# Long convolutions of a fused block: last frequency columns in four column groups of TensorE, 9-row products in the middle of each tile, odd halves first, and the inverse's 64-row products in both row halves

## What is computed

```
def fft_long_conv(u, spec, skip):
    L = u.shape[1]
    uf = u.astype(jnp.float32)
    y = jnp.fft.irfft(jnp.fft.rfft(uf, n=2 * L, axis=1) * spec[None], n=2 * L, axis=1)[:, :L]
    return (y + uf * skip.astype(jnp.float32)).astype(u.dtype)
...
    for n in range(HYENA_ORDER):
        gate = u[..., (n + 1) * D_HYENA:(n + 2) * D_HYENA]
        z = gate * fft_long_conv(z, spectra[:, n], skip[n])
```

## Time and profile before

| | us |
|---|---|
| median of three runs | 3216.32 (3215.01 to 3219.29) |
| the profiled execution, device time | 3212.31 |
| its span, first to last instruction | 3210.6 |
| TensorE busy in the span | 2982.2 (93%) |
| VectorE / ScalarE / GpSimd busy | 1142.0 / 779.5 / 900.5 |
| mean granted TensorE clock | 0.973 of full speed |

### The profile page before, as it was taken

How to read it: one execution, slowest core, us unless ns; L and a number is a source line. 1 busy time by engine, 2 the same in 40 slices (tenths; PEclk the granted TensorE clock), 3 DMA queues, 4 the chain that set the end, 5 groups by cost and what they waited for, 6 DMA issues and landing times.

```text
span 3210.6 us, 39686 instructions
## 1 busy us (share of the span) xinstructions
PE 2982.2 (93%) x15996; PEld 1985.1 (62%) x15996; DVE 1142.0 (36%) x1865; ACT 779.5 (24%) x1104; POOL 900.5 (28%) x744
## 2 busy tenths in 40 slices
PE   6999999999999999999999999999888888888887
PEld 4777778878788667887779794455333333333333
DVE  4566585661620154224152675513111011111112
ACT  2435542232322233223143621111000000000001
POOL 2342534455354314444424230001111111111110
PEclk9999999999999999999999999999999999899999
DMA  7324354542222212223312121047999999999997
GB/s 260 92 80 134 130 183 170 196 135 76 86 92 93 78 40 79 92 92 111 86 53 87 42 85 56 1 170 274 407 413 423 411 407 416 403 413 402 409 404 291
DMA packets 256000, 631.61 MB, mean 197 GB/s; under 512 B 19217, under 2 KB 208690, under 8 KB 230525
## 3 DMA queue, kind: packets, MB, share of 16 engines
q1 hardware_dynamic: 245053, 619.23, 51.6%
q0 software_dynamic: 10240, 8.43, 0.8%
q10 hardware_dynamic: 576, 2.10, 0.2%
HBM read 633.88 MB, written 20.97 MB: 204 GB/s over the span
## 4 chain that ended last, share of the span: by engine, by line
PE 63%; DMA 19%; DVE 6%; issue 5%; PEld 3%; ACT 2%; POOL 2%; SPq 0%; PEldq 0%; DVEq 0%; POOLq 0%; ACTq 0%
DMA arena<-in_w_up 18%; PE ps L545 12%; PE ps L547 12%; PE ps L546 11%; PE ps L4277 9%; PE ps L3480 2%; POOL ring_parts L427 2%; PE ps L3710 1%; PE ps L4294 1%; PE ps L2520 1%; PE ps L2519 1%; PE ps L2518 1%; PEld ps L545 1%; PEld ps L547 1%; PE ps L2670 1%
## 5 line engine op out<-in xcount | busy, mean ns | idle before, releaser
L427 POOL TENSOR_TENSOR ring_parts<-ring,arena_parts 128x512 fp32r<-128x512 f32 x544 | 720.7, 1358 | 1006.6 <-ACT arena_parts L401 772.5
L545 PE MATMUL ps<-arena_parts,arena_parts 128*128 128x512 f32 (+1 forms) x2012 | 749.7, 373 | 8.3 <-DVE arena_parts L536 4.2
L547 PE MATMUL ps<-arena_parts,ring_parts 128*128 128x512 f32 (+1 forms) x2012 | 741.2, 368 | 0.0
L4277 PE MATMUL ps<-arena 128*64 128x512 f32 x1008 | 500.1, 654 | 140.3 <-DMA arena<-in_w_up 95.4
L546 PE MATMUL ps<-hT_parts,arena_parts 128*128 128x512 f32 (+1 forms) x1648 | 596.0, 362 | 0.0
L4278 PE MATMUL ps<-arena 128*64 128x512 f32 x1008 | 501.3, 655 | 0.0
L4277 PEld LDWEIGHTS ps<-arena 128*64 128x64 f32 x1008 | 146.1, 150 | 462.5 <-issue 460.7
L545 PEld LDWEIGHTS ps<-arena_parts,arena_parts 128*128 128x128 f32 x2012 | 378.5, 188 | 85.2 <-issue 7.5
L547 PEld LDWEIGHTS ps<-arena_parts,ring_parts 128*128 128x128 f32 x2012 | 378.9, 188 | 69.1
L401 ACT ACTIVATE arena_parts<-ring 128x2048 fp32r<-128x2048 f32 (+1 forms) x103 | 207.0, 2013 | 634.4 <-PE ps L547 594.1
L546 PEld LDWEIGHTS ps<-hT_parts,arena_parts 128*128 128x128 f32 x1648 | 309.6, 188 | 49.9 <-issue 0.2
(11 more groups left out here) (623 smaller groups left out, 3623.2 us busy)
## 6 DMA issues: line engine op xcount, KB each, us to landing
arena<-in_w_down SPq DMA_DIRECT2D x64, 2048.0 KB, 23.1
arena<-in_w_gate SPq DMA_DIRECT2D x62, 2048.0 KB, 17.9
arena<-in_w_up SPq DMA_DIRECT2D x62, 2048.0 KB, 22.3
ring<-in_ffn_up SPq DMA_DIRECT2D x44, 1024.0 KB, 5.0
arena<-in_ada_w SPq DMA_DIRECT2D x14, 2048.0 KB, 9.9
ring<-in_ret_w_in SPq DMA_DIRECT2D x24, 1024.0 KB, 5.3
ring<-in_ffn_down SPq DMA_DIRECT2D x16, 1408.0 KB, 6.9
ring<-in_gdn_w_in SPq DMA_DIRECT2D x16, 1024.0 KB, 5.6
```

What stands on the lines that cost most here:

```text
L427: ins = pool.tensor_tensor(lower[:, at], whole[:, at], upper[:, at], ALU.subtract)
L545: pe.matmul(out, upper[:, r], self.upper[r][:, part], start=(r == 0), stop=False)
L547: ins = pe.matmul(out, lower[:, r], self.upper[r][:, part], start=False, stop=(r == self.tiles - 1))
L4277: pe.matmul(k.ps[upper, 2 + u, :], m.xeT[u][:, r, :], m.w_up[b][:, r, :], start=(r == 0), stop=(r == KD - 1))
```

## The change

- `transform_last` writes the four parts q to four groups of 32 PSUM partitions (q = 0, 1 in the first bank, partitions 0 to 63; q = 2, 3 in the second, partitions 64 to 127), in place of two groups twice. All eight 128-row products come first and then the four 9-row ones. For z it uses banks 2 and 3 in place of 0 and 1. ACT and DVE read the second bank at partitions 64 to 127.
- `transform_tile` does the odd parts first, then all four 9-row products, then the even parts. The wait for the even banks stands in front of the 9-row products. The odd parts signal after the 9-row products. Tile 0 of z does all four 9-row products first, in one group.
- The `unread_products` in steps 3 and 4 (5, 3 and 8 products for each order) are gone. Those before the gating waits stay.
- ACT and DVE take odd before even. DVE's first product waits only for the odd half of the filter's tile 1.
- The inverse's two 64-row products of a channel column lie in partitions 0 to 63 and 64 to 127 and are issued one behind the other, ahead of the 128-row products.

```diff
-        back_last[0:LAST, to] = parts[even].T[2 * P:]
-        back_last[GROUP:GROUP + LAST, to] = parts[odd].T[2 * P:]
+        back_last[2 * GROUP * to:2 * GROUP * to + LAST, to] = parts[even].T[2 * P:]
+        back_last[2 * GROUP * to + GROUP:2 * GROUP * to + GROUP + LAST, to] = parts[odd].T[2 * P:]
...
-    def transform_part(self, pe, m, odd, out, of, last, done):
+    def main_rows(self, pe, m, odd, out, of, first):
 
         at = slice(m * P, (m + 1) * P)
         for q in (odd, 2 + odd):
+            for t in range(2):
+                ins = pe.matmul(out(q), self.dft[:, q, t, at], of(q)[:, t, :], start=(first and t == 0), stop=(not first and t == 1))
+        return ins
+
+    def last_rows(self, pe, m, out, last, ends):
+
+        at = slice(m * P, (m + 1) * P)
+        for q in (1, 3, 0, 2):
             rows = slice(GROUP * q, GROUP * q + LAST)
...
+    def transform_tile(self, pe, m, out, of, last, done, evens_free):
+
+        self.main_rows(pe, m, 1, out, of, True)
+        pe.wait_ge(*evens_free)
+        self.last_rows(pe, m, out, last, True).then_inc(done, 1)
+        self.main_rows(pe, m, 0, out, of, False).then_inc(done, 1)
+
+    def transform_last(self, pe, bank, of, last):
+
+        at = slice(2 * P, N_COL)
+        parts = [(q, self.k.ps[GROUP * q:GROUP * (q + 1), bank + q // 2, :]) for q in range(4)]
+        for t in range(2):
+            for q, out in parts:
+                pe.matmul(out, self.dft[:, q, t, at], of(q)[:, t, :], start=(t == 0), stop=False)
+        for q, out in parts:
...
             pe.wait_ge(k.sem("hy_filtered"), 3 * i + 3)
             self.transform_last(pe, 0, filt, self.filt_last).then_inc(k.sem("hy_transformed"), 1)
-            k.unread_products(pe, 3, 5)
-            pe.wait_ge(k.sem("hy_spectrum"), 5 * i + 1)
-            self.transform_tile(pe, 0, lower, filt, self.filt_last, k.sem("hy_transformed"))
+            self.transform_tile(pe, 0, lower, filt, self.filt_last, k.sem("hy_transformed"), (k.sem("hy_spectrum"), 5 * i + 1))
             pe.wait_ge(k.sem("hy_spectrum"), 5 * i + 2)
-            k.unread_products(pe, 0, 3)
-            pe.wait_ge(k.sem("hy_spectrum"), 5 * i + 3)
-            self.transform_tile(pe, 1, lower, filt, self.filt_last, k.sem("hy_transformed"))
+            self.transform_tile(pe, 1, lower, filt, self.filt_last, k.sem("hy_transformed"), (k.sem("hy_spectrum"), 5 * i + 3))
             pe.wait_ge(k.sem("hy_spectrum"), 5 * i + 4)
-            self.transform_last(pe, 0, z, self.z_last).then_inc(k.sem("hy_z_transformed"), 1)
-            pe.wait_ge(k.sem("hy_spectrum"), 5 * i + 5)
-            k.unread_products(pe, 2, 8)
-            pe.wait_ge(k.sem("hy_product"), 5 * i + 2)
-            self.transform_tile(pe, 1, upper, z, self.z_last, k.sem("hy_z_transformed"))
+            self.transform_last(pe, 2, z, self.z_last).then_inc(k.sem("hy_z_transformed"), 1)
+            pe.wait_ge(k.sem("hy_product"), 5 * i + 1)
+            self.transform_tile(pe, 1, upper, z, self.z_last, k.sem("hy_z_transformed"), (k.sem("hy_product"), 5 * i + 2))
...
-                        for y in range(2):
-                            out = k.ps[:, 2 * (c % 2) + y, 0:FOLD]
-                            if m == 0:
-                                mm(out, self.prod_last[0:2 * GROUP, y, at], self.back_last[0:2 * GROUP, y], start=True, stop=False)
+                        outs = [k.ps[:, 2 * (c % 2) + y, 0:FOLD] for y in range(2)]
+                        if m == 0:
+                            for y, out in enumerate(outs):
+                                rows = slice(2 * GROUP * y, 2 * GROUP * (y + 1))
+                                mm(out, self.prod_last[rows, y, at], self.back_last[rows, y], start=True, stop=False)
+                        for y, out in enumerate(outs):
...
-            dve.wait_ge(k.sem("hy_transformed"), 5 * i + 5)
-            for odd in range(2):
-                dve.wait_ge(k.sem("hy_z_transformed"), 5 * i + 2)
-                dve.wait_ge(k.sem("hy_spectrum"), 5 * i + odd + 2)
+            dve.wait_ge(k.sem("hy_z_transformed"), 5 * i + 2)
+            for n, odd in enumerate((1, 0)):
+                dve.wait_ge(k.sem("hy_transformed"), 5 * i + 4 + n)
+                dve.wait_ge(k.sem("hy_spectrum"), 5 * i + 2 + n)
                 self.product(dve, do, 0, odd).then_inc(k.sem("hy_product"), 1)
```

More of the change, by code:

```diff
@@ L3688, in spectrum @@
         return self.Pq[rows, d, n] if n < 4 else self.Pq_last[rows, d]
-    def transform_part(self, pe, m, odd, out, of, last, done):
+    def main_rows(self, pe, m, odd, out, of, first):
         at = slice(m * P, (m + 1) * P)
         for q in (odd, 2 + odd):
-            rows = slice(GROUP * q, GROUP * q + LAST)
[L3695 to L3706, removed]
-        for odd in range(2):
[L3708 to L3711, removed]
+            for t in range(2):
+                ins = pe.matmul(out(q), self.dft[:, q, t, at], of(q)[:, t, :], start=(first and t == 0), stop=(not first and t == 1))
@@ new lines, in main_rows @@
+        return ins
+    def last_rows(self, pe, m, out, last, ends):
+        at = slice(m * P, (m + 1) * P)
+        for q in (1, 3, 0, 2):
+            rows = slice(GROUP * q, GROUP * q + LAST)
+            ins = pe.matmul(out(q), self.dft_last[rows, at], last[rows, :], start=(not ends or q % 2 == 0), stop=(ends and q % 2 == 1))
+        return ins
+    def transform_tile(self, pe, m, out, of, last, done, evens_free):
[3 more added lines that the diff above has]
+        self.main_rows(pe, m, 0, out, of, False).then_inc(done, 1)
@@ L3721, in transform_last @@
+        for t in range(2):
             for q, out in parts:
-                rows = slice(GROUP * q, GROUP * q + LAST)
-                ins = pe.matmul(out, self.dft_last[rows, at], last[rows, :], start=False, stop=True)
+                pe.matmul(out, self.dft[:, q, t, at], of(q)[:, t, :], start=(t == 0), stop=False)
+        for q, out in parts:
+            rows = slice(GROUP * q, GROUP * q + LAST)
+            ins = pe.matmul(out, self.dft_last[rows, at], last[rows, :], start=False, stop=True)
@@ L3861, in vector @@
                 self.weights_now(dve, 1)
-            dve.wait_ge(k.sem("hy_transformed"), 5 * i + 5)
-            for odd in range(2):
-                dve.wait_ge(k.sem("hy_z_transformed"), 5 * i + 2)
-                dve.wait_ge(k.sem("hy_spectrum"), 5 * i + odd + 2)
+            dve.wait_ge(k.sem("hy_z_transformed"), 5 * i + 2)
+            for n, odd in enumerate((1, 0)):
+                dve.wait_ge(k.sem("hy_transformed"), 5 * i + 4 + n)
+                dve.wait_ge(k.sem("hy_spectrum"), 5 * i + 2 + n)
                 self.product(dve, do, 0, odd).then_inc(k.sem("hy_product"), 1)
             dve.wait_ge(k.sem("hy_z_transformed"), 5 * i + 3)
-            dve.wait_ge(k.sem("hy_spectrum"), 5 * i + 5)
-            rows = slice(0, 2 * GROUP)
-            a, b = k.ps[rows, 0, :], k.ps[rows, 1, :]
+            rows, beyond = slice(0, 2 * GROUP), slice(2 * GROUP, 4 * GROUP)
+            a, b = k.ps[rows, 2, :], k.ps[beyond, 3, :]
             p, q = self.spectrum(rows, 0, 4), self.spectrum(rows, 1, 4)
@@ L3879, in vector @@
                 of = slice(GROUP * odd, GROUP * (odd + 1))
-                dve.tensor_tensor(self.prod_last[of, odd], e[of], q[of], ALU.subtract)
-                ins = dve.tensor_tensor(self.prod_last[of, 1 - odd], f[of], p[of], ALU.add)
+                to = [slice(GROUP * (odd + 2 * y), GROUP * (odd + 2 * y + 1)) for y in range(2)]
+                dve.tensor_tensor(self.prod_last[to[odd], odd], e[of], q[of], ALU.subtract)
+                ins = dve.tensor_tensor(self.prod_last[to[1 - odd], 1 - odd], f[of], p[of], ALU.add)
             ins.then_inc(k.sem("hy_product"), 1)
-            for odd in range(2):
-                dve.wait_ge(k.sem("hy_z_transformed"), 5 * i + odd + 4)
+            for n, odd in enumerate((1, 0)):
+                dve.wait_ge(k.sem("hy_z_transformed"), 5 * i + 4 + n)
+                dve.wait_ge(k.sem("hy_spectrum"), 5 * i + 4 + n)
                 self.product(dve, do, 1, odd).then_inc(k.sem("hy_product"), 1)
@@ L3910, in scalar @@
                 act.activation(to, k.ps[:, 6 + n % 2, :], ACT.Copy).then_inc(k.sem("hy_z"), 1)
-            for done, (n, rows) in enumerate(((4, slice(0, 2 * GROUP)), (0, slice(0, P)), (2, slice(0, P)), (1, slice(0, P)), (3, slice(0, P)))):
+            for done, (n, rows) in enumerate(((4, slice(0, 2 * GROUP)), (2, slice(0, P)), (0, slice(0, P)), (3, slice(0, P)), (1, slice(0, P)))):
                 act.wait_ge(k.sem("hy_transformed"), 5 * i + done + 1)
                 for d in range(2):
-                    ins = act.activation(self.spectrum(rows, d, n), k.ps[rows, 2 * (n // 2) % 4 + d, :], ACT.Identity, scale=self.wk[rows, n:n + 1])
+                    of = slice(rows.start + d * 2 * GROUP, rows.stop + d * 2 * GROUP) if n == 4 else rows
```

(1 more changed line is left out.)

7 lines of the change are left out of this document (4 added, 3 removed).

## The result

| | before | after |
|---|---|---|
| median (range), us | 3216.73 (3215.01 to 3219.29) | 3189.71 (3189.03 to 3190.97) |
| profiled execution, us | 3212.31 | 3190.39 |
| TensorE busy, us | 2982.2 | 2957.3 |
| convolutions, first `filter_last` to the output projection, us | 172.28 | 147.74 |

Both medians are of four runs. The ratio is 0.9917, 95% interval 0.9905 to 0.9929: 27.0 us saved, and 23 to 31 by the interval. The convolutions alone are 172.28 - 147.74 = 24.5 us shorter. The profiled executions differ by less, 21.9, since the stages ahead were 1.8 us quicker and those behind took 4.4 longer (1116.5 against 1112.1). The tail belongs to no kernel: over the eleven changed kernels traced for this study it lies anywhere from 1112.9 to 1117.7, and not in the order of what was changed (1113.1 for `rows_first_b`, 1115.4 for `after_again`).

A forecast was written before the change was run, and what follows sets the result against it. PE was taken to bound the convolutions, then DVE's chain before m = 1. 25.8 us saved less 2.6 for clock falls leaves 23.2: 3212.31 becomes 3189.1, plus 4.0 for the median gives 3193; range 3187 to 3204.

The forecast's parts named there:

- S to the first 64-row product: From the start of the filter's last columns to PE's being ready for the inverse: 30.14 us in place of 40.59.
- DVE's first product behind S: DVE's first product starts when filter tile 1's odd half ends, 15.67 us after the filter's last columns start.
- DVE's chain: 32 DVE operations without a break, 20.10 us, becoming the limit before the inverse's m = 1; PE waits 0.4 us.
- m = 1 to the next m = 1, order 0: In the inverse, the second m = 1 comes 11.45 us behind the first, against 12.33 before: 0.9 us saved.
- wait before the filter's last columns: PE's wait for DVE's fold, once in each order, grows from 0.81 to about 1.9 us.
- clock falls: Without unread products, the wait at the filter's last columns may lower PE's clock: one fall or two short, 2.6 us lost.
- saved at full clock: Convolutions: 12.5 us saved in order 0 and 13.3 in order 1, together 25.8 us.
- Column groups not four at a time (1): Last columns cost 4.7 us or more in place of 2.82, up to 11.3 less saved, giving 3204; chance 6%.
- 64-row pairs not side by side (4): The inverse's paired 64-row products don't overlap, 5.2 us less saved, giving 3198; chance 5%.
- A gain that does not reach the end (3): Expert weights end last; if their stream held its time, the result would be 3216; chance 3%.
- A clock that falls and stays (2): PE stays at 1.2 GHz in the convolutions, up to 35.8 us more in each order, giving 3262; chance 2%.
- Edits at nothing: Tile 0 of z loses a 9-row group (1.06 us of PE); partition moves and odd-before-even taken as free: 0 gained.

The follow-up runs named there:

- rows_first_b: Changed kernel with the filter's second product rows moved ahead of the odd half of z's tile 0; median 3185.39 us, ratio 0.9899.
- after_again: The changed kernel run once more, unaltered, on the chip of three other follow-up kernels; median 3189.78 us, ratio 0.9925.
- dve_longer: Changed kernel with three more unread 64x512 DVE operations in each order, ahead of the last frequencies; median 3196.84 us, ratio 0.9941.
- two_groups: Changed kernel with the last columns written in two column groups, twice, as before; median 3198.11 us, ratio 0.9952.
- old_inverse_b: Changed kernel with both of the inverse's 64-row products kept in partitions 0 to 63, as before; median 3195.18 us, ratio 0.9933.
- order_only: Kernel before with the new order and no unread products, but last columns in two groups and the old inverse; median 3202.81 us, ratio 0.9961.
- no_unread_b: Kernel before without its 5, 3 and 8 unread products in each order, nothing else changed; median 3227.47 us, ratio 1.0030.
- cols_only_b: Kernel before with one edit, the last columns in four column groups; median 3215.04 us, ratio 0.9992.

## Why the prediction was right

The forecast was 3193 us, measured were 3189.7. Step by step:

| step | foretold | measured |
|---|---|---|
| last columns, start to start | 2.82 | 2.84 |
| S to the first 64-row product | 30.14 | 30.49 |
| DVE's first product behind S | 15.67 | 15.87 |
| DVE's chain | 20.10 | 20.42 |
| S to the first m = 1 | 35.8 | 36.34 |
| waits at m = 1 and at the second gate | 0.4, 0.6 | 0.52, 0.65 |
| channel column of the inverse | 2.62 | 2.63 |
| m = 1 to the next m = 1, order 0 | 11.45 | 11.49 |
| wait before the filter's last columns | 1.9 | 1.86 |
| clock falls | 2.6 | 0 |
| saved at full clock | 25.8 | 24.5 |
| first load of expert weights | 2082 to 2085 | 2079.91 |

**What binds.** That PE sets the time up to DVE's chain, and that DVE takes over just before m = 1, is shown by the rows, by `dve_longer`, and by the waits at m = 1 that are gone in `two_groups` and `old_inverse_b`. This part of the mechanism was right.

**The sum.** It was 1.3 us too high. I took DVE and ACT at partitions 64 to 127 at 0 with 0.07 us per operation as the upper end. The eight operations for the last frequencies now take 5.42 us, where they took 5.11, 0.3 more, and the chain starts 0.2 later behind S than worked out. Both are in front of m = 1 and count in both orders, 1.1 us together. The variants split the 0.3: with only the reads at partitions 64 to 127 (`old_inverse_b`) the eight take 5.23 us, with only the writes elsewhere (`two_groups`) 5.31, and with neither (`order_only`) 5.12. Of the 0.2, half is PE's: four 128-row products between groups of other shape take 3.63 us (1948.59 to 1952.22), where 3.53 was put. The rest is 0.1 us more between the next group's start on PE and DVE's. The three tiles from S to the inverse take 24.80 us where 24.5 were put; with 0.05 for the two last columns, that is the 0.35 us by which the first 64-row product comes later than worked out. A slip of the sum is small: 8.8 + 2.62 gives 11.4 and not 11.45.

**The clock.** This term was wrong: 2.6 us were taken off for one fall or two, and none came. The row that I went by, a fall behind a 1.8 us wait in the first block, was no guide to a wait of 1.86 us here. In eight traces with that wait in both orders, it stood sixteen times, never with a fall behind it. Windows of the changed kernel, the wait and the last columns behind it:

```profile
1943.90:1945.70 1.80, 0.00 (x0) 0.00 (x0) 1.73 (x4) 0.00 (x0) 0.00 (x0) 1.00 0.00 0
1945.75:1948.59 2.84, 2.84 (x24) 0.57 (x24) 1.23 (x2) 0.00 (x0) 0.00 (x0) 1.00 0.03 6
```

The two errors, 1.3 and 2.6 us, are opposite in sign and left the prediction of the stretch 1.3 us short of what was saved (23.2 against 24.5). That the whole came as near as 3 us is in part luck. The forecast also added 4.0 us, by which the median before lay above the profiled execution; after the change it lies 0.7 us below. That takes 4.7 us off, the convolutions take off 1.3 and the stages ahead 1.8, and the stages behind put 4.4 on: 3193.1 becomes 3189.7.

**The rivals.** Column groups not four at a time (1) and 64-row pairs not side by side (4) are refuted by the rows. A gain that does not reach the end (3) is too: expert loads start 27.6 us earlier, and the median fell by 27.0. A clock that falls and stays (2) did not come, but falls that pass do occur: `no_unread_b` is slower than before by them, 6.8 us in its profile. I had named the effect of the unread products on the clock, but looked for it only in the new order's waits.

**Edits at nothing.** That z's tile 0, one 9-row group shorter, would gain nothing because of DVE's fold held: the wait is 1.86 us. I named the wait but took it as given; `rows_first_b` shows that one moved line removes it.

## What to carry to other kernels

The worth of a part depends on which wait stands behind it: the same four column groups gave 0.5 us in the old order, 5.6 without its clock falls by the estimate, and 9.6 in the new one. So a change in parts is judged in both orders, before the first part is thrown out, and a kernel whose runs spread with the clock is not judged by one profile. Put the first half of the next tile, whose banks are free, in front of a wait for a copy, rather than filler; filler that covers a real wait may be holding the clock, as here in the old order, and is taken out only together with the wait. And a wait that one has predicted and accepted is the next thing to remove.

## What the hardware showed that I had not expected

- Length of a wait does not tell whether the clock falls. Behind 1.36 us, in both orders of `no_unread_b`, the granted clock went to 0.50 for 3.41 us, behind 1.45 us in the same kernel not, and behind 1.86 us, sixteen times, not. In front of the waits with falls PE had done last columns, or those and unread products of 128 columns; in front of the 1.45 us and the 1.86 us it had done at least eight passes of 128x128x512. Waits of 2.08 us (`no_unread_b`) and 2.80 us (`cols_only_b`) also had a fall behind them, in both orders. `no_unread_b` and `cols_only_b` have one profile each, and what made the difference was not tried alone.
- A granted clock of 0.50 lasted 3.41 us in five of the six falls in the convolutions of these traces and 6.83 us in one.
- Sixteen passes of 128 rows by 32 columns in four column groups take 1.85 us in fp32, with other data in each, where eight passes in two groups take 1.84. Two 64-row products in the two row halves take 0.65 us, where one takes 0.64.
